# Two fused transformer blocks: the first FFN's up outputs in pairs by Strassen's scheme

## The chip, the cores and the metric

The kernel is one program on one core of a Trainium2 chip. The core has TensorE (matmuls, in the profile PE, with its weight loads as PEld), VectorE (DVE), ScalarE (ACT), GpSimd (POOL) and SyncE (SP), each with its own queue of instructions that it works off in order. They share SBUF; matmuls write to PSUM, which has eight banks of 128 partitions x 512 fp32 numbers. The metric is the device time of one execution in microseconds (us), and lower is better.

## The reference, cut to what matters

Two transformer blocks in float32 on 512 tokens of width 1024, one behind the other. The change touches the FFN of the first block and the last addition of the second:

```python
h2 = rms_norm(x, norm2_w[l])
x = x + jnp.square(jax.nn.relu(h2 @ ffn_w1[l])) @ ffn_w2[l]      # first block: 1024 -> 4096 -> 1024
...
f = (jax.nn.silu(h @ ffn_w_gate[l]) * (h @ ffn_w_up[l])) @ ffn_w_down[l]
x = x + rmsnorm(f, norm_ffn_post[l])                             # second block, the end of the program
```

`rms_norm` divides each token by the root of the mean square over its 1024 channels and multiplies by a gain per channel.

## The kernel before, in words

**Three passes.** Activations lie with channels on the partitions and tokens in the columns, in chunks of 128 channels: `x_sb` is eight chunks of 128 x 512. A float32 product is made of three fast ones. Each operand is split into a high part (a rounded copy, type fp32r) and a low part (the original minus the high one), and `mm3` issues high x high, high x low, low x high into one bank (L834 is the line of every matmul).

**Weights.** SyncE loads slots of 128 x 1024 into `w_raw` (three buffers). GpSimd writes the high part of a slot (L2512) and the low part (L2517, in this part of the program in four pieces of 256 columns) into a ring of three slots, `w_hi_t` and `w_lo_t`. A slot is split once TensorE has finished with the slot three before it (`BEHIND`), and raw buffers come free with the low part.

**The first FFN.** It runs in two halves of 16 chunks. An up chunk (`fm(("up1", half, c))`) takes one slot: 8 channel blocks x 3 passes = 24 matmuls of 512 columns. Its input is not normed: `u2_hi` and `u2_lo` hold x times the gain, and the factor of each token, `r_h`, is multiplied in when the bank is emptied, on VectorE with the ReLU (L2007, into `r1`, whose two chunks take turns). ScalarE squares (L1561) and writes the high part `hid1_hi` (L1562), VectorE the low part `hid1_lo` (`hidden_low`, L1857). Behind 16 up chunks stand eight down chunks (`down1`), each 16 blocks x 3 passes over two slots, which VectorE adds to `x_sb` (L2090).

**The end.** The last FFN ends with eight down chunks summed in `merged_t` (called `f_acc`), the last one in two parts in one bank. Then come the sum of squares through a matmul with ones, logarithm and exponential on ScalarE (L1473, L1476, by token halves), VectorE's product with gain and factor (L2420), the addition to x on TensorE, VectorE and GpSimd, and the DMAs of the result.

**What sets the order.** `plan()` writes one list of steps, `ORDER`. The block of each engine walks through that list and issues its own part of each step, so the order on an engine is the order of the list and of the code of a step. Engines meet by semaphores: `did(...)` counts up behind an instruction, `after(...)` gives the value to wait for, and `own` is a wait on a result of the same engine. `take` picks the bank that has been filled longest ago and waits until it is empty; `release` says so.

## Time and profile before

| | us |
|---|---|
| median of 3 runs | 1781.65 |
| the runs | 1780.2 to 1781.75 |
| the profiled execution, its own time | 1781.87 |
| its span, first to last instruction | 1780.1 |

| engine | busy us | share of the span |
|---|---|---|
| TensorE, matmuls | 1758.4 | 99% |
| GpSimd | 1118.7 | 63% |
| VectorE | 753.0 | 42% |
| ScalarE | 491.5 | 28% |

The mean granted TensorE clock is 0.999 of full speed. Durations of single matmuls overlap, so what one costs is read from the distance of their starts. The profile puts helper functions under one line, and buffer numbers are left out of names: `hid_lo` is `hid1_lo`, `u_hi` is `u2_hi`, `r` is `r1`, `bank` is any of the eight.

### The profile page before, as it was taken

The page shows a single profiled execution, that of the slowest core. Times are in us where ns is not written, and L with a number is a line of the kernel's source. Part 1 is how long each engine was busy: PE and PEld are TensorE (multiplying, and loading weights), DVE is VectorE, ACT ScalarE, POOL GpSimd, SP SyncE. Part 2 cuts the span into 40 slices and gives each one's busy share as a digit, 9 for nine tenths or more (in the row PEclk, how much of TensorE's full clock was granted, in tenths as well). Part 3 has the DMA queues.
Part 4 walks back from the last instruction along what each step waited for, and adds up shares of the span by engine and source line. Part 5 has one row for each costly group of instructions (what it writes and reads, how often), then busy time and mean ns, then how long its engine had stood idle before and what let it go on. Part 6 is the DMA issues. An engine that isn't in the chain of part 4 may idle for free.

```text
span 1780.1 us, 22414 instructions
## 1 busy us (share of the span) xinstructions
PE 1758.4 (99%) x8502; PEld 1417.1 (80%) x8502; DVE 753.0 (42%) x1266; ACT 491.5 (28%) x937; POOL 1118.7 (63%) x1181
## 2 busy tenths in 40 slices
PE   8999999999999999999999999999999999999998
PEld 5776768888888887878888888777888888888886
DVE  6348656320122244262006373545433586215532
ACT  3236653210021111222014232554300222222222
POOL 6643648777777786667766665555788574444442
PEclk9999999999999999999999999999999999999999
DMA  6620012332222223222232222212223232222331
GB/s 218 209 74 28 25 56 99 100 102 95 95 95 96 97 83 126 73 82 96 95 99 74 77 75 83 72 61 71 83 95 107 71 107 95 95 95 96 100 100 59
DMA packets 47001, 162.88 MB, mean 91 GB/s; under 512 B 5582, under 2 KB 6670, under 8 KB 46640
## 3 DMA queue, kind: packets, MB, share of 16 engines
q1 hardware_dynamic: 45688, 158.28, 26.6%
q10 hardware_dynamic: 1208, 3.18, 0.6%
q8 instruction: 68, 1.11, 0.3%
q14 instruction: 37, 0.30, 0.1%
HBM read 158.41 MB, written 2.11 MB: 90 GB/s over the span
## 4 chain that ended last, share of the span: by engine, by line
PE 93%; DVE 3%; ACT 1%; issue 1%; DMA 0%; POOL 0%; ACTq 0%; SPq 0%; DVEq 0%; POOLq 0%
PE bank L834 92%; DVE sq_sum L1847 1%; PE bank L1222 1%; PE bank L1176 1%; DMA x_sb<-in_x 0%; DVE tmp L1852 0%; DVE h_lo L1910 0%; ACT sq L1435 0%; POOL w_lo_t L2517 0%; ACT att_pt L1693 0%; ACT att_l_t L1680 0%; DVE sq_parts L1880 0%; ACT h_hi L1547 0%; ACT sb_e L1752 0%; DVE tmp L2215 0%
## 5 line engine op out<-in xcount | busy, mean ns | idle before, releaser
L2517 POOL TENSOR_TENSOR w_lo_t<-w_raw,w_hi_t 128x256 fp32r<-128x256 f32 (+1 forms) x892 | 820.8, 948 | 168.2 <-ACT w_hi_t L1513 149.8
L2512 POOL TENSOR_SCALAR w_hi_t<-w_raw 128x1024 fp32r<-128x1024 f32 (+1 forms) x221 | 241.2, 1091 | 430.6 <-PE bank L834 395.2
L834 PE MATMUL bank<-h_hi,w_hi_t 128*128 128x512 f32 x1044 | 418.6, 401 | 9.3 <-ACT h_hi L1547 8.5
L834 PE MATMUL bank<-h_hi,w_lo_t 128*128 128x512 f32 x1044 | 407.4, 390 | 0.0
L834 PE MATMUL bank<-h_lo,w_hi_t 128*128 128x512 f32 x1044 | 402.8, 389 | 0.2 <-DVE h_lo L1910 0.2
L834 PEld LDWEIGHTS bank<-h_hi,w_hi_t 128*128 128x128 f32 x1044 | 197.0, 189 | 61.7 <-issue 19.9
L834 PEld LDWEIGHTS bank<-h_lo,w_hi_t 128*128 128x128 f32 x1044 | 195.8, 188 | 42.6 <-issue 1.7
L834 PEld LDWEIGHTS bank<-h_hi,w_lo_t 128*128 128x128 f32 x1044 | 197.1, 189 | 40.7 <-issue 1.2
L834 PE MATMUL bank<-hid_hi,w_hi_t 128*128 128x512 f32 x432 | 168.0, 389 | 0.0
L834 PE MATMUL bank<-hid_lo,w_hi_t 128*128 128x512 f32 x432 | 168.0, 389 | 0.0
L834 PE MATMUL bank<-hid_hi,w_lo_t 128*128 128x512 f32 x432 | 168.0, 389 | 0.0
L834 PE MATMUL bank<-u_hi,w_hi_t 128*128 128x512 f32 x280 | 108.9, 389 | 0.0
L834 PE MATMUL bank<-u_hi,w_lo_t 128*128 128x512 f32 x280 | 108.9, 389 | 0.0
L834 PE MATMUL bank<-u_lo,w_hi_t 128*128 128x512 f32 x280 | 108.9, 389 | 0.0
L1513 ACT ACTIVATE w_hi_t<-w_raw 128x1024 fp32r<-128x1024 f32 x52 | 55.0, 1060 | 187.6 <-PE bank L834 187.5
L834 PEld LDWEIGHTS bank<-hid_hi,w_hi_t 128*128 128x128 f32 x432 | 81.1, 188 | 17.0
L834 PEld LDWEIGHTS bank<-hid_lo,w_hi_t 128*128 128x128 f32 x432 | 81.1, 188 | 16.8
L834 PEld LDWEIGHTS bank<-hid_hi,w_lo_t 128*128 128x128 f32 x432 | 81.1, 188 | 16.8
L1561 ACT ACTIVATE r<-r 128x512 f32<-128x512 f32 x32 | 20.2, 632 | 214.9 <-DVE r L2007 214.9
L834 PE MATMUL bank<-o_hi,w_hi_t 128*128 128x512 f32 x192 | 75.8, 395 | 0.0
L834 PE MATMUL bank<-o_lo,w_hi_t 128*128 128x512 f32 x192 | 74.8, 390 | 0.0
L834 PE MATMUL bank<-o_hi,w_lo_t 128*128 128x512 f32 x192 | 74.8, 390 | 0.0
(364 smaller groups left out, 2509.9 us busy)
## 6 DMA issues: line engine op xcount, KB each, us to landing
w_raw<-in_w SPq DMA_DIRECT2D x276, 512.0 KB, 3.2
y<-in_w SPq DMA_DIRECT2D x6, 512.0 KB, 4.8
x_sb<-in_x SPq DMA_DIRECT2D x4, 512.0 KB, 7.5
out_y<-x_sb SPq DMA_DIRECT2D x8, 256.0 KB, 2.4
x_sb<-in_x ACTq DMA_DIRECT2D x1, 1536.0 KB, 6.8
u_raw<-in_w SPq DMA_DIRECT2D x2, 512.0 KB, 5.9
toep<-table SPq DMA_DIRECT2D x4, 256.0 KB
decay<-in_decay SPq DMA_DIRECT2D x1, 1024.0 KB, 4.9
```

The costliest lines, as they stand in the source:

```text
L834: return pe.matmul(out, lhs, rhs, start=start, stop=stop, **kw)
L1176: last = pe.transpose(out[:, b * P:(b + 1) * P], att_row(u)[0][:, b * P:(b + 1) * P], ident[:])
L1222: last = pe.transpose(out[:, 256 * hf + b * P:256 * hf + (b + 1) * P], row[:, b * P:(b + 1) * P], ident[:])
L1513: act.activation(w_hi[RING[i]], w_raw[:, n % RAW], ACT.Copy).then_inc(*did("wa_hi", i))
L1561: chain(act.activation(r1[:, n % 2], r1[:, n % 2], ACT.Square))
L1847: dve.tensor_tensor(sq_sum[0:parts, 0:cols], b[0] if c == 1 else sq_sum[0:parts, 0:cols], b[1], ALU.add).then_inc(*did("sq_v", key, c))
L2512: pool.tensor_scalar(hi[:, 0:cols], raw[:, 0:cols], 1.0, 0.0, ALU.mult, ALU.add).then_inc(*did("w_hi", i))
L2517: ins = pool.tensor_tensor(lo[:, piece], raw[:, piece], hi.bitcast(F32)[:, piece], ALU.subtract)
```

## The change

**Alone and in pairs.** The first eight up chunks of half 0 stay as they are (`N_ALONE`). The other 8 of half 0 and all 16 of half 1 are made two at a time: four pairs and eight pairs. A pair's output is two chunks x 512 tokens, seen as 2 x 2 quarters: upper and lower chunk, left and right 256 tokens. The input is seen as 2 x 2 as well, channels 0 to 511 and 512 to 1023 by token halves, and so is the weight. By the form of Strassen's scheme used here, seven products of quarters do instead of eight. A product is 4 blocks x 3 passes = 12 matmuls of 256 columns.

**Inputs.** Sums of inputs need real, normed ones, since the token factor differs from left to right. VectorE writes `x_norm` (`st_norm`), four sums `x_sums` of it (`st_sum`), and ScalarE and VectorE split them (`st_split`) into `h_hi` and `h_lo`. Three plain input quarters are split behind the last single chunk (`st_x`, `st_x_rest`). All of this stands between the single chunks 2 to 7 and in front of the first pair.

**Weights.** Four of the seven products use sums of weight quarters. VectorE makes them in four banks (`sums`), ScalarE writes their high parts (`sum_hi`), VectorE their low parts (`sum_lo`). The three plain quarters are split by GpSimd (`raw_quarter`). The ring is now counted in half slots (`place_weights`); a fourth raw buffer `w_more` is used for pairs.

**Outputs.** ScalarE copies the first product out (`pair_p6`). VectorE adds the third to it (`u2_t`), adds the second (`q_t`), and the three quarters `pair_c22`, `pair_c12`, `pair_c21`; the fifth, sixth and seventh products add onto banks that these have read. ScalarE makes the ReLU, square and copy of each chunk (`pair_left`, `pair_right`), GpSimd the low part (`hidden_low`), which VectorE made before; the last pair's stand between the first down slots.

**The end of the program.** The last down chunk is done by token halves in two banks (`down_halves`), so that the left half's norm and addition are issued while TensorE works on the right half.

```diff
     for half in range(2):
-        for c in range(half == 0, HALF1):
+        alone = range(1, N_ALONE) if half == 0 else ()
+        for c in alone:
+            if c == N_ALONE - 1:
+                run([("st_pre", ("pair", 0, N_ALONE)), ("st_x",)])
             fm(("up1", half, c))
+            run([("st_" + what,) for what, at in (("norm", 2), ("sum", 3), ("split", 4)) if c == at])
+        if half == 0:
+            put(("st_x_rest",))
+        for c in range(N_ALONE * (half == 0), HALF1, 2):
+            lin(("pair", half, c), "pair", 2)
         down(("down1", half), HALF1, "pre")
+        if half == 0:
+            order.insert(len(order) - 1, ("st_pre", ("pair", 1, 0)))
...
+    Q_S2, Q_S1, Q_W11, Q_S3, Q_W12, Q_S4, Q_W22 = range(7)
+    X_OF = {Q_S2: T2, Q_S1: T1, Q_W11: X11, Q_S3: T3, Q_W12: X21, Q_S4: X22, Q_W22: T4}
+    BANK_OF = {Q_S2: "b", Q_S1: "c", Q_W11: "a", Q_S3: "d", Q_W12: "a", Q_S4: "c", Q_W22: "d"}
...
+            elif stage == "pair":
+                name = step[1]
+                for m in range(7):
+                    x, spot = X_OF[m], (name, BANK_OF[m])
+                    out = (take(spot) if m < 4 else ps(spot))[:, 0:T // 2]
+                    pe.wait_ge(*after("st_lo" if m in (Q_S1, Q_S2, Q_S3, Q_S4) else "w_lo", name, m))
+                    if m == Q_W12:
+                        pe.wait_ge(*after("st_u2", name))
+                    elif m == Q_S4:
+                        pe.wait_ge(*after("st_q", name))
+                    elif m == Q_W22:
+                        pe.wait_ge(*after("st_c22", name))
...
+                    for k in range(4):
+                        wsl = slice(k * P, (k + 1) * P)
+                        xh, xl = x_quarter(k, x)
+                        last = mm3(out, wh[:, wsl], wl[:, wsl], xh, xl, k == 0 and m < 4, k == 3, skip_group_check=True)
...
+        def sum_hi(name, s):
+            m = Q_OF_S[s]
+            act.wait_ge(*after("st_s", name, {1: 2, 2: 4, 3: 3, 4: 4}[s]))
+            act.wait_ge(*slot_done[BEHIND[(name, m)]])
+            act.activation(quarter(name, m)[0], s_of(name, s), ACT.Copy).then_inc(*did("st_hi", name, m))
...
+        def pair_phase(pairs):
+            sum_hi(pairs[0], 4)
+            for old, new in zip(pairs, pairs[1:]):
+                pair_p6(old)
+                sum_hi(new, 2)
+                sum_hi(new, 1)
+                sum_hi(new, 3)
+                pair_left(old)
+                sum_hi(new, 4)
+                pair_right(old)
...
+        def pair_inner(name):
+            dve.wait_ge(*after("st_pe", name, Q_W11))
+            dve.wait_ge(*evacuated((name, "b")))
+            dve.tensor_tensor(u2_t, pair_bank(name, "a"), p6_t, ALU.add).then_inc(*did("st_u2", name))
+            own("st_u2", name)
+            dve.tensor_tensor(q_t, u2_t, pair_bank(name, "c"), ALU.add).then_inc(*did("st_q", name))
...
+            for old, new in zip(pairs, pairs[1:]):
+                sums(new)
+                sum_lo(new, 2)
+                pair_inner(old)
+                sum_lo(new, 1)
+                pair_c22(old)
+                sum_lo(new, 3)
+                pair_c12(old)
+                pair_c21(old)
+                sum_lo(new, 4)
...
+            since += 1
+            if n and PAIR_SLOT[i] is not None and since in (2, 3):
+                hidden_low(PAIR_SLOT[i], since - 2)
...
+                for hf, chunks in enumerate((range(KD), (0, 1, 4, 2, 5, 3, 6, 7))):
+                    side = halves_t[hf]
+                    own("rstd", "fpost", hf)
+                    for c in chunks:
+                        if c == KD - 1:
+                            dve.wait_ge(*after("last_c", hf))
+                        dve.scalar_tensor_tensor(out=f_acc[:, c, side], in0=f_acc[:, c, side], scalar=col("fpost", c),
+                                                 in1=ps(("ms", "fpost", hf))[:, 0:T // 2], op0=ALU.mult, op1=ALU.mult)\
+                           .then_inc(*did("last_t", hf, c))
```

VectorE, from the bank of single chunk 2 on. In the kernel before, each chunk has two instructions:

```order
L2007 SCALAR_TENSOR_TENSOR r<-bank,r_h 128x512 [waits bank_full7,hid]
L1857 TENSOR_TENSOR hid_lo<-r,hid_hi 128x512 [waits hid_s]
L2007 SCALAR_TENSOR_TENSOR r<-bank,r_h 128x512 [waits bank_full6,hid]
L1857 TENSOR_TENSOR hid_lo<-r,hid_hi 128x512 [waits hid_s]
L2007 SCALAR_TENSOR_TENSOR r<-bank,r_h 128x512 [waits bank_full3,hid]
```

The same place in the changed kernel, up to the low parts of the input sums:

```order
L2364 SCALAR_TENSOR_TENSOR r<-bank,r_h 128x512 [waits bank_full7,hid]
L2099 TENSOR_TENSOR hid_lo<-r,hid_hi 128x512 [waits hid_s]
L2094 SCALAR_TENSOR_TENSOR x_norm<-x_sb,par,r_h 128x512 [waits hid]
L2094 SCALAR_TENSOR_TENSOR x_norm<-x_sb,par,r_h 128x512 x7
L2364 SCALAR_TENSOR_TENSOR r<-bank,r_h 128x512 [waits bank_full6]
L2099 TENSOR_TENSOR hid_lo<-r,hid_hi 128x512 [waits hid_s]
L2217 TENSOR_TENSOR x_sums<-x_norm 128x1024 [waits st_h,hid]
L2217 TENSOR_TENSOR x_sums<-x_norm 128x1024
L2217 TENSOR_TENSOR x_sums<-x_norm,x_sums 128x1024 [waits st_t] x2
L2364 SCALAR_TENSOR_TENSOR r<-bank,r_h 128x512 [waits bank_full3]
L2099 TENSOR_TENSOR hid_lo<-r,hid_hi 128x512 [waits hid_s]
L2221 TENSOR_TENSOR h_lo<-x_sums,h_hi 128x1024 [waits st_xhi,hid]
```

The norms, sums and low parts of the input stand between the chunks' own instructions, and all later ones of VectorE come behind them.

VectorE in one round of the pairs, in the changed kernel, with buffer numbers. Banks 0, 5, 1 and 7 hold the sums of weights; banks 4, 2, 6 and 3 hold the products; `st_pe` counts products of TensorE:

```order
L2123 TENSOR_TENSOR bank0<-w_raw 128x512 [waits st_lo,w_landed2]
L2125 TENSOR_TENSOR bank5<-bank0,w_raw 128x512 [waits st_lo,st_s,w_landed0]
L2127 TENSOR_TENSOR bank1<-w_raw,bank5 128x512 [waits st_lo,st_s]
L2129 TENSOR_TENSOR bank7<-w_raw,bank5 128x512 [waits st_lo]
L2136 TENSOR_TENSOR w_lo_t<-bank5,w_hi_t 128x512 [waits st_hi]
L2144 TENSOR_TENSOR tmp<-bank4,tmp 128x256 [waits bank_free3,st_pe]
L2146 TENSOR_TENSOR tmp<-tmp,bank2 128x256 [waits st_u2]
L2136 TENSOR_TENSOR w_lo_t<-bank0,w_hi_t 128x512 [waits st_hi]
L2152 TENSOR_TENSOR r1<-tmp,bank6 128x256 [waits st_q,st_pe,hid]
L2136 TENSOR_TENSOR w_lo_t<-bank1,w_hi_t 128x512 [waits st_hi]
L2157 TENSOR_TENSOR r1<-tmp,bank2 128x256 [waits st_pe,hid]
L2161 TENSOR_TENSOR r1<-tmp,bank6 128x256 [waits st_pe]
```

The four sums of the next pair (the first four rows) stand in front of the inner sum of the running pair (`tmp<-bank4,tmp`), for which the fifth product waits.

ScalarE in the same round, changed kernel. `w_hi_t<-bank` are the high parts of the next pair's sums, `r` and `hid_hi` belong to the running pair:

```order
L1724 ACTIVATE tmp<-bank 128x256 [waits st_pe,st_u2]
L1700 ACTIVATE w_hi_t<-bank 128x512 [waits st_pe,st_s] x3
L1705 ACTIVATE r<-bank 128x256 [waits st_pe,hid_p]
L1707 ACTIVATE r<-r 128x256 [waits bank_free2]
L1709 ACTIVATE r<-r 128x512 [waits bank_free4,s_chain]
L1710 ACTIVATE hid_hi<-r 128x512 [waits s_chain]
L1700 ACTIVATE w_hi_t<-bank 128x512 [waits st_pe,st_s]
L1714 ACTIVATE r<-r 128x512 [waits bank_free6]
L1715 ACTIVATE r<-r 128x512 [waits s_chain]
L1716 ACTIVATE hid_hi<-r 128x512 [waits s_chain]
```

The high part of the fourth sum stands behind the four instructions of the running pair's left chunk; before the change ScalarE had two instructions per up chunk, and none on weights here.

## Rows read from the trace of the kernel before

**Rows 1.** The page: busy times of the engines

```profile
PE 1758.4 (99%) x8502; PEld 1417.1 (80%) x8502; DVE 753.0 (42%) x1266; ACT 491.5 (28%) x937; POOL 1118.7 (63%) x1181
```

**Rows 2.** The chain that ended last: start us, us, what

```profile
278.22 511.89 PE bank L834 x2240
...
1767.74 0.48 ACT rstd_t L1473
...
1775.50 0.60 ACT x_sb L1803
```

**Rows 3.** Timeline, TensorE, 512 columns: start us, us, engine, line, names, shapes

```profile
340.00 0.39 PE L834 MATMUL bank<-u_hi,w_hi_t 128*128 128x512 f32 x1
...
343.85 0.39 PE L834 MATMUL bank<-u_hi,w_lo_t 128*128 128x512 f32 x1
...
349.07 0.39 PE L834 MATMUL bank<-u_lo,w_hi_t 128*128 128x512 f32 x1
```

**Rows 4.** Timeline, TensorE, 256 columns

```profile
1397.05 0.28 PE L834 MATMUL bank<-m_hi,w_lo_t 128*128 128x256 f32 x1
...
1398.85 0.28 PE L834 MATMUL bank<-m_hi,w_lo_t 128*128 128x256 f32 x1
```

**Rows 5.** Timeline, VectorE: up outputs of chunks 2 and 7 leave their banks

```profile
317.50 0.69 DVE L2007 SCALAR_TENSOR_TENSOR r<-bank,r_h 128x512 f32<-128x512 f32 x1 [4.15 <-PE bank L834]
...
344.35 0.69 DVE L2007 SCALAR_TENSOR_TENSOR r<-bank,r_h 128x512 f32<-128x512 f32 x1 [3.80 <-PE bank L834]
```

**Rows 6.** Groups of VectorE by shape, 278 to 790 us: busy, mean ns

```profile
L1857 DVE TENSOR_TENSOR hid_lo<-r,hid_hi 128x512 fp32r<-128x512 f32 x32 | 32.8, 1025 | 0.7 <-ACT hid_hi L1562 0.7
...
L2007 DVE SCALAR_TENSOR_TENSOR r<-bank,r_h 128x512 f32<-128x512 f32 x32 | 22.1, 692 | 122.0 <-PE bank L834 119.5 <-ACT r_h L1496 2.5
...
L2319 DVE TENSOR_TENSOR ret_a_t<-bank,decay 128x256 f32<-128x256 f32 x3 | 1.2, 415 | 0.0
```

**Rows 7.** Groups of ScalarE by shape, same stretch

```profile
L1561 ACT ACTIVATE r<-r 128x512 f32<-128x512 f32 x32 | 20.2, 632 | 214.9 <-DVE r L2007 214.9
...
L1581 ACT ACTIVATE sig<-bank 128x512 f32<-128x512 f32 x6 | 3.6, 598 | 64.2 <-PE bank L834 64.2
```

**Rows 8.** Groups of GpSimd by shape, whole span

```profile
L2517 POOL TENSOR_TENSOR w_lo_t<-w_raw,w_hi_t 128x256 fp32r<-128x256 f32 x826 | 651.0, 818 | 17.3
...
L2512 POOL TENSOR_SCALAR w_hi_t<-w_raw 128x1024 fp32r<-128x1024 f32 x220 | 240.6, 1094 | 425.5 <-PE bank L834 395.2 <-DVE h_lo L1910 20.9 <-DMA w_raw<-in_w 9.3
...
L2512 POOL TENSOR_SCALAR w_hi_t<-w_raw 128x512 fp32r<-128x512 f32 x1 | 0.6, 617 | 5.1 <-DMA w_raw<-in_w 5.1
```

**Rows 9.** Busy time of each engine, 656.27 to 676.00 us

```profile
core 0: us, PE busy (x) PEld busy (x) DVE busy (x) ACT busy (x) POOL busy (x), PEclk, DMA share, GB/s
656.27:676.00 19.73, 19.73 (x89) 16.34 (x88) 19.03 (x17) 6.34 (x9) 18.45 (x18) 1.00 0.40 148
```

**Rows 10.** Timeline, GpSimd: a weight slot split beside an idle and a busy VectorE

```profile
644.74 2.82 POOL L2517 TENSOR_TENSOR w_lo_t<-w_raw,w_hi_t 128x256 fp32r<-128x256 f32 x4
...
661.75 4.49 POOL L2517 TENSOR_TENSOR w_lo_t<-w_raw,w_hi_t 128x256 fp32r<-128x256 f32 x4
...
666.20 1.50 POOL L2512 TENSOR_SCALAR w_hi_t<-w_raw 128x1024 fp32r<-128x1024 f32 x1
```

**Rows 11.** Timeline, ScalarE, end of the program

```profile
1768.24 0.42 ACT L1476 ACTIVATE rstd_t<-rstd_t 128x256 f32<-128x256 f32 x1
```

**Rows 12.** Timeline, VectorE, end of the program

```profile
1768.69 0.48 DVE L2420 SCALAR_TENSOR_TENSOR sig<-merged_t,par,rstd_t 128x256 f32<-128x256 f32 x1 [7.71 <-ACT rstd_t L1476]
...
1774.65 0.69 DVE L2426 TENSOR_TENSOR x_sb<-x_sb,bank 128x512 f32<-128x512 f32 x1
```

**Rows 13.** Timeline, TensorE, behind a gap

```profile
234.83 1.25 PE L1176 MATMUL bank<-ident,x_sb 128*128 128x128 f32 x8 [2.20 <-DVE x_sb L2217]
```

**Rows 14.** TensorE behind that gap: stretch, its length, busy, granted clock

```profile
237.00:238.00 1.00, 1.00 (x7) 0.50 0.06 16
...
240.00:241.00 1.00, 1.00 (x8) 1.00 0.00 0
```

More of the change, by code:

```diff
@@ L47 @@
 RAW = 3
+N_ALONE = 8
 SPL = 3
@@ L366 @@
             LAST_USE[SLOTS[name][0]] = n
+    elif step[0] == "pair":
+        LAST_USE.update({(step[1], m): n for m in range(7)})
     elif step[0] == "down":
@@ L722, in h_free @@
                 last = (step[2], NT - 1)
-        if last is not None:
+            elif step[0] == "pair":
+                last = step[1]
+        if last in PAIR_LIST:
+            eng.wait_ge(*after("st_pe", last, 6))
+        elif last is not None:
             eng.wait_ge(*full(last))
@@ L915, in _ @@
                     fill(("tab", n), mm(out[0:NH, :], rb[rows], onehot[rows], True, True))
-            elif stage == "norm" and step[1] != "post":
+            elif stage == "norm" and step[1] not in ("post", "fpost"):
                 ms(step[1], len(norms[step[1]][0]))
@@ L1060, in _ @@
                 nm = (name[0], name[1], o)
[L1061 to L1066 removed]
+                if name[0] == "down2" and o == KD - 1:
+                    down_halves(nm, nk, i0)
+                    continue
+                out = take(nm)
                 for k in range(nk):
@@ new lines, in sum_lo, with pair_bank @@
+        def sum_lo(name, s):
+            m = Q_OF_S[s]
+            own("st_hi", name, m)
+            hi, lo = quarter(name, m)
+            dve.tensor_tensor(lo, s_of(name, s), hi.bitcast(F32), ALU.subtract).then_inc(*did("st_lo", name, m))
+        def pair_bank(name, b):
+            return ps((name, b))[:, 0:T // 2]
+        def pair_inner(name):
[4 more added lines that the diff above has]
+            dve.tensor_tensor(q_t, u2_t, pair_bank(name, "c"), ALU.add).then_inc(*did("st_q", name))
@@ L1861, in _, with x_lo @@
+        def x_lo(n):
+            c0, side = (X11, X21, X22)[n]
+            own("st_xhi", n)
+            blocks = [(0, 4, u2_lo05[:, 0:4])] if c0 == 0 else [(4, 6, u2_lo05[:, 4:6]), (6, 8, u2_lo67[:])]
+            for k0, k1, lo in blocks:
+                ins = dve.tensor_tensor(lo[:, :, side], h_norm[:, k0:k1, side], u2_hi[:, k0:k1, side].bitcast(F32),
+                                        ALU.subtract)
+            ins.then_inc(*did("st_xlo", n))
         for i, v in enumerate(EPS_VAL):
@@ L2551, in _ @@
             name = step[1]
-            if stage in ("fm", "tm", "cmp_up", "out_end") or (stage == "down" and step[3] == 0):
+            if stage in ("fm", "tm", "cmp_up", "out_end", "pair") or (stage == "down" and step[3] == 0):
                 first, count = SLOTS[name]
```

450 lines of the change are left out of this document (358 added, 92 removed).

## The prediction

> **What bounds the kernel now.** I read the page first: TensorE is busy for 99% of the span, the other engines for 28 to 63% [rows 1]. The reader is to see that TensorE work taken away is time taken away, as long as nobody makes TensorE wait. The chain of waits says the same of the stretch in question: from 278.22 us it runs through 511.89 us of matmuls without a break [rows 2], and the whole first FFN (up chunks and down chunks) lies inside. So the change is worth the matmul time it removes, minus every wait that it puts into a stretch that has none today. The program then ends with a piece that is not TensorE: from 1767.74 us the chain is ScalarE and VectorE work on the last norm, and its last piece begins at 1775.50 us [rows 2].
>
> Next I took prices. Matmuls of 512 columns start 9.07 us apart over 40 intervals (340.00 to 349.07), which is 0.227 us each [rows 3]. Matmuls of 256 columns start 1.80 us apart over 15 intervals, 0.120 us each, and not half of 0.227 [rows 4]. Both streams are at full clock. A part of about 0.013 us per matmul does not shrink with the columns.
>
> **The pairs on TensorE.** Two up chunks are 48 matmuls of 512 columns, 48 x 0.227 = 10.88 us. A pair is 7 products x 4 blocks x 3 passes = 84 matmuls of 256 columns, 84 x 0.120 = 10.08 us (1.44 us a product). The gain is 0.80 us a pair, 7% and not an eighth. With 12 pairs that is 9.6 us, if nothing waits. The Trainium skill (TensorE: Matmul & The Clock Gate, section Back-to-back issue gap) gives columns / 2.4 + 2.5 ns, which would be 0.109 and 0.216 us and 1.2 us a pair. The trace has 0.120 and 0.227, and the sum goes by those.
>
> **The loop through the pairs.** What stands between pairs is a ring through three engines, and I price it from rows. A VectorE instruction of 512 columns that reads a bank takes 0.69 us and one of 256 columns 0.415; one that reads two SBUF tensors beside a busy GpSimd takes 1.03 on average [rows 6]. ScalarE takes 0.63 from SBUF and 0.60 from a bank for 512 columns [rows 7], and 0.42 for 256 [rows 11]. A result of TensorE is taken up 0.27 us after the next matmul could have started: the last matmul of chunk 7 starts at 343.85, the next is due at 344.08, and VectorE begins at 344.35 [rows 3, 5]. Other hand-overs I take at 0.04.
> From the order of the instructions: when the sixth product (S4) of a pair ends, VectorE makes the upper right quarter (0.27 + 0.42). ScalarE then does ReLU 0.42, square 0.63 and copy 0.63, and only behind these the high part of the next pair's fourth sum, 0.60: 2.4 us with hand-overs. VectorE takes its low part (0.69) and then makes the four sums of the pair after that, which depend on each other: about 1.0 + 3 x 0.69 = 3.1. ScalarE takes the high part of the second sum (0.64, it waits for the fourth), VectorE its low part (0.72), and only then the inner sum of the running pair (0.42), for which the fifth product waits. Fifth and sixth product follow, 2.88. Round trip: 0.69 + 2.4 + 0.73 + 3.1 + 0.68 + 0.72 + 0.44 + 0.16 + 2.88 = 11.8 us. A pair can't be faster than this ring, so in steady state it takes 11.8 us against 10.88 before: **0.9 us lost a pair**, where TensorE alone would win 0.8. Four pairs have two such rounds and eight have six; the first and last pair of a phase are outside. The price of the write of a sum into a bank is in no row; with 0.69 for every sum the ring is 11.5, with 1.0 for every sum 12.7. I take 11.8, since three of the four read only one SBUF tensor.
> GpSimd would not be worse than that: per pair three quarters (0.62 + 2 x 0.71 to 0.82 each) and two low parts of the hidden (2 x 0.71 to 0.82 each) [rows 8, 10] are 9.0 to 10.1 us with nothing added, inside 11.8.
>
> **The set-up before the first pair.** This is the largest term. Today VectorE has only 0.69 + 1.03 us in 5.44 us of each up chunk [rows 5, 6]. The changed kernel puts between chunks 2 and 7: eight normed chunks, four sums and four low parts of 1024 columns, four weight sums and three low parts, in front of the chunks' own work. VectorE is then a queue without a gap while GpSimd splits weights, and a later stretch shows what that means: 17 instructions in 19.03 us, 1.12 each, both engines busy nearly throughout [rows 9]; in such a stretch GpSimd's four pieces take 4.49 instead of 2.82 [rows 10]. A 1024-column instruction stands in no row: 256 columns cost 0.415 and 512 cost 0.69, so 1.25 alone, and 1.68 with one wait of 0.43 for GpSimd; two of 1.12 would be 2.24. I take 1.68, since it follows the two shapes that have rows. The Trainium skill (SBUF — State Buffer, section SBUF: two separate sides) says that the loser of the shared ports waits for a whole instruction of the winner, which gives one wait and 1.68; a shared rate would give 2.24, and the eight would cost 4.5 us more. No row here decides between them.
> From 317.50 [rows 5]: bank and low part 1.81, norms 8 x 1.12 = 9.0, 1.81, sums 6.7, 1.81, low parts 6.7, 3.6, which is 348.9. Weight sums 2.8 (GpSimd is idle by then), ScalarE 0.64, low part 0.7: 353.1. TensorE has finished chunk 7 at 344.1, so the first product is **9.0 us late**. The next three products run to 358.9. VectorE meanwhile: two low parts 1.4, first input quarter 1.5, bank and low part of chunks 7 and 6 1.4, four more pieces 2.8, 0.7, low part 0.7, the next pair's sums 2.8, ScalarE 0.64, 0.7, inner sum 0.42: 366.1. The fifth product is **7.2 us late**. A gap also costs clock: after a wait of 2.20 us [rows 13] the granted clock was 0.50 in 237 to 238 us and 1.00 again in 240 to 241 [rows 14], i.e. 1.2 GHz for some 3.5 us. Behind the second gap that is 1.7 us more; behind the first it disappears in the second.
>
> **The ends of the phases.** The hidden low parts of the last pair go to GpSimd, between the first down slots. GpSimd comes out of the ring 6.9 us after the last pair's start, splits a slot in 4.2 (1.05 + 4 x 0.78), and TensorE is due at 10.1: about 1.2 us late. Then come one slot, one hidden part (1.6), one slot, and the other hidden part: 23.2, where TensorE needs it at 11.4 + 45 x 0.227 = 21.6. Together 2.9 us a phase, 0 at the least.
>
> **The tail.** The last down chunk of both halves has 66 matmuls of 256 columns instead of 33 of 512: 7.92 for 7.48, so 0.9 us more. In return the left half's norm is done before TensorE ends: VectorE needs 8 x 0.42 + 0.43 = 3.8 us behind its factor instead of 6.65 (1768.69 to 1775.34) [rows 12], and ScalarE has two instructions instead of four ahead of that (0.85). Net -2.5; bounds -4 and +0.9.
>
> **Sum.** First phase: 9.0 + 7.2 + 1.7 + 2 x 0.92 - 2 x 0.80 + 2.9 = 21.0. Second phase: sums wait for the last down chunk, first pair 1.1 late, so +0.3, then 6 x 0.92 - 0.80 + 2.9: 7.9 in all. Tail -2.5. Together +26.4 on the profiled execution's 1781.87 us (span 1780.1): 1808.3. The median of the runs is 1781.65, so I forecast 1808.
>
> **Rivals.**
> Faster (1770): the ring does not bind, since VectorE and ScalarE have slack on average (VectorE has some 8 us in 10.08), and the set-up hides. Then 12 x 0.80 + 2.5 are won, 1769.8. For it: those averages, and five products of lead in the weight buffers. Against it: averages do not shorten a chain, and the order puts the next pair's sums in front of the running pair's inner sum. It decides if the ring is below 10.1 us and VectorE's queue ends before 344.
> Only the set-up costs (1788): pairs run at 10.08, ends cost nothing, +17.9 - 9.6 - 2.5 = +5.8.
> No contention in the set-up (1799): at 0.69 and 1.25 VectorE's queue is done at 344, the 9.0 us vanish, 1808 - 9. Against it: the 1.12 us of such a stretch [rows 9].
> Clock (1822): every wait of 1.1 to 1.8 us in the pairs lowers TensorE to 1.2 GHz as the one of 2.20 did [rows 13, 14]. The products behind it are on the ring, 8 x 1.7 more.
>
> **How the numbers follow.** Forecast 0.50, no contention 0.17, only the set-up 0.10, clock 0.08, faster 0.12, and 0.03 that gains and losses cancel. A measurement can tell 0.2% (3.6 us) from no change. Faster by more 0.12, within 0.03, slower 0.85. The range takes in all the slower cases: from 1788 up to 1824, the top being the clock case with a little contention on top. Without the slower cases' spread the forecast's own range is 1800 to 1816.
>
> **What would show it.** In the profile after: VectorE without a gap from 318 to about 366 us; TensorE waiting twice behind it there, for w_lo_t and for tmp, 9 and 7 us; then once in nearly each pair, 1.8 us, for tmp; pairs 11.8 us apart, products of twelve matmuls 1.44 us long; a wait for hid_lo by GpSimd at the first down chunk. Wrong if pairs stand 10.1 us apart (the ring), if the first product starts by 345 us (contention), or if VectorE's 1024-column instructions take over 2 us.

## The result, and the profile after

| | before | after |
|---|---|---|
| median, us | 1780.93 (1779.7 to 1781.75, 4 runs) | 1801.87 (1800.25 to 1802.46, 4 runs) |
| ratio | | 1.0115, 95% interval 1.0103 to 1.0127 |
| profiled execution, span, us | 1780.1 | 1800.2 |

The change makes the kernel slower by 20.9 us. The forecast was 1808, 26.4 over its profiled execution. The page after, against [rows 1]:

```profile
PE 1755.1 (97%) x9000; PEld 1438.0 (80%) x9000; DVE 831.2 (46%) x1404; ACT 541.4 (30%) x1040; POOL 1143.9 (64%) x1223
```

The reader is to see that TensorE's busy time fell by only 3.3 us while its share fell from 99 to 97%: the loss is waiting. Who is waited for shows in TensorE's waits (us in total, times, longest):

```profile
PE bank L953 <- issue: 13.8, 2, 8.3
PE bank L953 <- DVE tmp L2144: 9.5, 9, 1.2
```

**The set-up.** The two "issue" waits are those ahead of the first pair's first and fifth product. (A figure in brackets behind a row is the idle time just before it, by the profile; waits taken from the distance of two starts come out 0.1 to 0.3 us longer.) The last matmul of chunk 7 starts at 345.23 (343.85 before, [rows 3]; 1.4 us of offset arose earlier in the program and is in every number from here on). TensorE was due with the first product at 345.46 and, after four products, with the fifth at 361.59:

```profile
353.91 0.55 PE L953 MATMUL bank<-h_hi,w_hi_t 128*128 128x256 f32 x1 [8.29 <-issue]
...
367.22 0.55 PE L953 MATMUL bank<-u_hi,w_hi_t 128*128 128x256 f32 x1 [5.47 <-issue]
```

"Issue" names nobody, since TensorE waits here for something that ended just before. VectorE's timeline of the same stretch names it:

```profile
320.21 9.44 DVE L2094 SCALAR_TENSOR_TENSOR x_norm<-x_sb,par,r_h 128x512 f32<-128x512 f32 x8
...
330.88 3.63 DVE L2217 TENSOR_TENSOR x_sums<-x_norm 128x1024 f32<-128x1024 f32 x2
334.43 3.44 DVE L2217 TENSOR_TENSOR x_sums<-x_norm,x_sums 128x1024 f32<-128x1024 f32 x2
...
340.86 5.72 DVE L2221 TENSOR_TENSOR h_lo<-x_sums,h_hi 128x1024 fp32r<-128x1024 f32 x4 [1.79 <-ACT h_hi L1749]
...
353.12 1.89 DVE L2136 TENSOR_TENSOR w_lo_t<-bank,w_hi_t 128x512 fp32r<-128x512 f32 x3 [0.66 <-ACT w_hi_t L1700]
355.04 1.23 DVE L2188 TENSOR_TENSOR u_lo<-x_norm,u_hi 128x1024 fp32r<-128x1024 f32 x1
...
357.50 3.88 DVE L2188 TENSOR_TENSOR u_lo<-x_norm,u_hi 128x512 fp32r<-128x512 f32 x4
...
366.09 0.69 DVE L2136 TENSOR_TENSOR w_lo_t<-bank,w_hi_t 128x512 fp32r<-128x512 f32 x1 [0.66 <-ACT w_hi_t L1700]
366.70 0.41 DVE L2144 TENSOR_TENSOR tmp<-bank,tmp 128x256 f32<-128x256 f32 x1
```

Apart from waits for ScalarE of 1.79, 0.66 and 0.66 us VectorE works from 318.9 to 367. The 1.79 us are a loop of its own: ScalarE writes the high parts of the input sums (`h_hi`) only from 339.71, behind a square and a copy of a single chunk whose bank VectorE itself had emptied at 337.80, late. The first low part that TensorE needs begins at 353.12, the inner sum `tmp` of the fifth product at 366.70.

**The ring.** Eight of the waits for `tmp` are 1.13 to 1.16 us and the ninth, at the start of phase 2, is 0.4. One round of VectorE, from one inner sum to the next:

```profile
534.24 0.41 DVE L2144 TENSOR_TENSOR tmp<-bank,tmp 128x256 f32<-128x256 f32 x1
...
538.02 0.42 DVE L2157 TENSOR_TENSOR r<-tmp,bank 128x256 f32<-128x256 f32 x1
...
540.81 0.69 DVE L2136 TENSOR_TENSOR w_lo_t<-bank,w_hi_t 128x512 fp32r<-128x512 f32 x1 [1.00 <-ACT w_hi_t L1700]
541.42 0.87 DVE L2123 TENSOR_TENSOR bank<-w_raw 128x512 f32<-128x512 f32 x1
...
543.72 0.69 DVE L2129 TENSOR_TENSOR bank<-w_raw,bank 128x512 f32<-128x512 f32 x1
545.08 0.69 DVE L2136 TENSOR_TENSOR w_lo_t<-bank,w_hi_t 128x512 fp32r<-128x512 f32 x1 [0.66 <-ACT w_hi_t L1700]
545.68 0.41 DVE L2144 TENSOR_TENSOR tmp<-bank,tmp 128x256 f32<-128x256 f32 x1
```

It takes 545.68 - 534.24 = 11.44 us, with the members in the order that the prediction gave them. TensorE's own 84 matmuls would take 10.08, so each round costs 1.36 us.

**The balance**, by marks in the two traces (the start of the same instruction in both), after against before: 1.4 us of offset ahead of the change; phase 1 (chunk 7's last matmul to the first down matmul) 61.4 against 43.8, +17.6; phase 2 89.4 against 87.0, +2.4; behind the phases about +0.7. The last long run of matmuls starts at 1461.32 and not 1439.21, 22.1 later, and the span ends 20.1 later: the tail gives 2.0. Without the offset the change costs 18.7 us by these marks (17.6 + 2.4 + 0.7 - 2.0). Its chain after ends so (start us, us, what):

```profile
1461.32 326.08 PE bank L953 x1487
1788.41 3.22 DVE merged_t L2768 x8
1791.63 1.29 DVE x_sb L2773 x2
1792.93 3.14 DVE merged_t L2768 x8
```

### The profile page after: what moved, and what is told of

Same layout as the page of the kernel before. It is cut to its first block, busy times and chain, and to the rows that moved or that the text cites. A ratio compares the mean times of both kernels' runs of the same rounds, so it can differ in the third digit from the quotient of the medians.

```text
span 1800.2 us, 23932 instructions
## 1 busy us (share of the span) xinstructions
PE 1755.1 (97%) x9000; PEld 1438.0 (80%) x9000; DVE 831.2 (46%) x1404; ACT 541.4 (30%) x1040; POOL 1143.9 (64%) x1223
## 3 DMA queue, kind: packets, MB, share of 16 engines
q8 instruction: 72, 1.18, 0.3%
## 4 chain that ended last, share of the span: by engine, by line
PE 64%; DVE 2%; POOL 1%; ACT 0%; issue 0%; DVEq 0%; ACTq 0%; POOLq 0%
PE bank L953 64%; DVE sq_sum L2089 1%; PE bank L1406 1%; POOL w_lo_t L2901 0%; DVE merged_t L2768 0%; POOL hid_lo L2852 0%; DVE tmp L2094 0%; POOL w_hi_t L2896 0%; DVE h_lo L2267 0%; DVE sq_parts L2237 0%; DVE x_sb L2773 0%; ACT sq L1615 0%; PE bank L1513 0%; POOL w_lo_t L2845 0%; DVE x_sb L2799 0%
## 5 line engine op out<-in xcount | busy, mean ns | idle before, releaser
L2901 POOL TENSOR_TENSOR w_lo_t<-w_raw,w_hi_t 128x256 fp32r<-128x256 f32 (+1 forms) x796 | 750.7, 971 | 167.0 <-ACT w_hi_t L1745 150.5
L953 PE MATMUL bank<-h_hi,w_hi_t 128*128 128x512 f32 (+1 forms) x1236 | 473.7, 383 | 17.4 <-ACT h_hi L1792 8.5
L953 PE MATMUL bank<-h_hi,w_lo_t 128*128 128x512 f32 (+1 forms) x1236 | 462.2, 374 | 0.0
L953 PE MATMUL bank<-h_lo,w_hi_t 128*128 128x512 f32 (+1 forms) x1236 | 457.9, 373 | 0.3 <-DVE h_lo L2267 0.3
L953 PE MATMUL bank<-hid_hi,w_hi_t 128*128 128x512 f32 (+1 forms) x454 | 172.5, 380 | 0.3
L953 PE MATMUL bank<-hid_hi,w_lo_t 128*128 128x512 f32 (+1 forms) x454 | 172.0, 379 | 0.0
L953 PE MATMUL bank<-hid_lo,w_hi_t 128*128 128x512 f32 (+1 forms) x454 | 172.0, 379 | 0.0
L953 PE MATMUL bank<-u_hi,w_hi_t 128*128 128x256 f32 (+1 forms) x232 | 76.7, 331 | 14.9 <-DVE tmp L2144 9.5
L953 PE MATMUL bank<-u_lo,w_hi_t 128*128 128x256 f32 (+1 forms) x232 | 75.9, 327 | 0.0
L953 PE MATMUL bank<-u_hi,w_lo_t 128*128 128x256 f32 (+1 forms) x232 | 75.8, 327 | 0.0
```

The source lines that it names most:

```text
L953: return pe.matmul(out, lhs, rhs, start=start, stop=stop, **kw)
L2901: ins = pool.tensor_tensor(lo[:, piece], src[:, piece], hi.bitcast(F32)[:, piece], ALU.subtract)
```

## The experiments

Where a run's profile is compared with another, distances between marks inside the program are used: the place of chunk 7's end differs by up to 3.3 us between the profiled executions, for reasons ahead of the change. "The 1787 kernel" is the first one below. All ratios are to the kernel before, beside runs of it on the same chip.

**1. VectorE's inner sum ahead of the low part (r1_dve).**

```diff
                 sums(new)
-                sum_lo(new, 2)
                 pair_inner(old)
+                sum_lo(new, 2)
```

> Edit: in a round of the pairs VectorE makes the inner sum of the running pair (tmp<-bank,tmp and the q behind it) before the low part of the next pair's second weight sum, not behind it. Ring theory (the round of 11.44 us is a ring: fourth weight sum's low part, four sums of the next pair, high part, low part, inner sum, fifth product, and back through ScalarE's left chunk): the wait for the high part and the low part (0.66 + 0.6 us) leave the ring, so its period falls from 11.44 to about 10.17 us, the same in all 9 rounds, and the gap before the first pair's fifth product shrinks by the same 1.27. Sum: 10 x 1.27 = 12.7 us off 1801.9, so 1789 us. Rival 1 (the round is bound by GpSimd, which splits three quarters and makes two low parts of the hidden activations per pair): period stays 11.4, time 1801 to 1802. Rival 2 (matmuls of 256 columns issue slower than 0.120 us over a long stretch): the same, no wait for tmp left but the distance of the starts grows.

1786.98 us, ratio 1.0031 (1.0019 to 1.0043). The same round in its profile:

```profile
532.15 0.42 DVE L2144 TENSOR_TENSOR tmp<-bank,tmp 128x256 f32<-128x256 f32 x1
...
534.14 0.41 DVE L2152 TENSOR_TENSOR r<-tmp,bank 128x256 f32<-128x256 f32 x1
```

The instruction at L2152 stands at 524.07 one round earlier, so a pair takes 10.07 us. No wait for `tmp` is left, and phase 2 takes 80.7 us, which is eight pairs at TensorE's own 10.08. The wait ahead of the first pair's fifth product fell too, by 1.6 us (distance 4.15 instead of 5.75; 1.27 was expected). The ring theory holds; GpSimd and the matmuls' rate fall as causes, since neither was touched.

**2. ScalarE's fourth high part first (r2_act), and 3. both edits (r3_both).**

```diff
-                pair_left(old)
                 sum_hi(new, 4)
+                pair_left(old)
                 pair_right(old)
```

> Edit: ScalarE writes the high part of the next pair's fourth weight sum before the running pair's left chunk (ReLU, ReLU, square, copy), not behind it. Ring theory: the high part then waits only for the seventh product, which frees its half slot 4.88 us behind the inner sum, instead of 5.89 us: the period falls by about 1.0 us to 10.4 to 10.5 us, and 9 rounds give 9 us: 1793 us. The first pair gains nothing. GpSimd rival: no change, 1802 us. Rival: the left chunk is now so late that its bank or r1 holds up a product; then a new wait of TensorE for bank a (the third product of the next pair) shows, and the time stays above 1797.

1800.67 us, ratio 1.0111 (1.0094 to 1.0127): far less than expected. The rounds take 10.96 us and not 10.4. ScalarE in one of them:

```profile
524.32 0.60 ACT L1700 ACTIVATE w_hi_t<-bank 128x512 fp32r<-128x512 f32 x1 [2.28 <-PE bank L953]
524.81 0.38 ACT L1705 ACTIVATE r<-bank 128x256 f32<-128x256 f32 x1
...
528.58 0.36 ACT L1724 ACTIVATE tmp<-bank 128x256 f32<-128x256 f32 x1
528.84 1.08 ACT L1700 ACTIVATE w_hi_t<-bank 128x512 fp32r<-128x512 f32 x2
```

The high part starts early, but then both chunks' ReLUs, squares and copies, 4.0 us from 524.81 to 528.84, stand between it and the next high part, for which VectorE waits (its sums are ready at 528.4). One ring was shortened and another, through ScalarE's queue, took its place 0.5 us below. There is a second cost: GpSimd's low parts of the hidden chunks wait for ScalarE's later copies (1.82 us, in front of 394.93), and the first down slot stands behind them. The slot is ready at 403.77, and TensorE starts with it at 403.88, 1.7 us late.

> Edit: both edits of the two kernels before. Ring theory: the ring is 11.44 - 1.27 - 1.0 = 9.2 us, shorter than the 84 matmuls of a pair at 0.120 us (10.08 us), so TensorE is the bound: period 10.08, no wait for tmp; 9 x 1.36 + 1.27 = 13.5 us off 1801.9, so 1788.4 us, and phase 2 (eight pairs) takes 80.6 us and not 89.4. If it does not reach 10.08, another ring (GpSimd's quarters, or ScalarE's left chunk and its bank) is behind this one, and its wait shows in TensorE's timeline.

1791.14 us, ratio 1.0058 (1.0043 to 1.0073). 1788.4 was expected. The pairs stand at 10.08 as expected, but that needed the first edit alone; what the second adds is the late down slot, 1.7 and 1.8 us at the ends of the two phases (distances 1.83 and 1.96 between the last and the first matmul, against 0.14). So this is slower than the first edit alone.

**4. The tail alone (tail_only).** The changed kernel with

```diff
+        for c in range(half == 0, HALF1):
+            fm(("up1", half, c))
+        down(("down1", half), HALF1, "pre")
```

in place of the loop with pairs, and VectorE's `hidden_low` of the last chunk put back.

> Edit: the changed kernel with all up chunks of the first FFN single as before (no pairs, no sums of inputs or weights); of the change only the last output chunk by token halves is left. Theory (the two parts add up): the pairs cost 23 us net and the tail gives 2.0 back, so this is 1780.9 - 2.0 = 1778.9 us, ratio 0.9989. Rival (the tail gives nothing or costs, and the pairs' net is only 20.9): 1780.9 us or more. Rival (tail gives the 2.5 us that the prediction's sum had): 1778.4 us. The profile should have TensorE at 0.227 us a matmul in the first FFN, and the last instruction 2 us earlier than before.

1779.7 us, ratio 0.9990 (0.9981 to 0.9999). From the start of the last long run of matmuls to the end of the span it takes 1778.1 - 1439.03 = 339.1 us, and before 1780.1 - 1439.21 = 340.9: 1.8 us, against 2.0 in the whole change, so the two parts add up within 0.2 us. The pairs' net is then 1801.9 - 1779.7 = 22 us.

**5. Less GpSimd beside the set-up (c1_quiet).** Three quarters of the low parts of the weights of chunks 3 to 7 are left out:

```diff
-            for k in range(0, cols if n == 0 else 1024, size):
+            quiet = i in [SLOTS[("up1", 0, c)][0] for c in range(3, N_ALONE)]
+            for k in range(0, cols if n == 0 else size if quiet else 1024, size):
```

> Edit: the changed kernel, with GpSimd writing only the first 256 of 1024 columns of the low parts of the weights of single chunks 3 to 7 (three quarters of that part of the computation are left out), so that it is idle for most of the time in which VectorE prepares the inputs. Contention theory (VectorE's instructions with two SBUF operands take 1.18 us, and 1.77 us with 1024 columns, because GpSimd works beside them): the eight normed chunks fall from 1.18 to about 0.70 us each and the four sums from 1.77 to about 1.3, 5.7 us less in VectorE's queue, and the wait of TensorE in front of the first pair falls from 8.7 to about 3 us: 1801.9 - 6 = 1796. Rival (the operations take this long by themselves; the queue alone makes the wait): durations and the wait stay, 1802.

1795.97 us, ratio 1.0083 (1.0070 to 1.0097), 5.9 us less. VectorE's added work in its timeline:

```profile
318.66 7.02 DVE L2094 SCALAR_TENSOR_TENSOR x_norm<-x_sb,par,r_h 128x512 f32<-128x512 f32 x8
...
326.91 3.21 DVE L2217 TENSOR_TENSOR x_sums<-x_norm 128x1024 f32<-128x1024 f32 x2
330.04 3.01 DVE L2217 TENSOR_TENSOR x_sums<-x_norm,x_sums 128x1024 f32<-128x1024 f32 x2
...
336.03 5.05 DVE L2221 TENSOR_TENSOR h_lo<-x_sums,h_hi 128x1024 fp32r<-128x1024 f32 x4 [1.78 <-ACT h_hi L1749]
```

2.4, 0.8 and 0.7 us less than after, 3.9 in all, and the first product comes 4.3 us earlier against chunk 7's end (4.4 instead of 8.7). Contention is real, and the part of it that this edit takes away is about half of that wait. It did not go away altogether (0.88 a norm and not 0.70), as GpSimd still writes high parts and the first pieces, so half is the least that contention costs here. What the wait would be with none is not shown: an estimate from the durations, 8 norms at 0.69, 4 sums and 4 low parts at 1.23 (what these shapes take where GpSimd is idle), has VectorE's queue 6.9 us shorter than after, which would leave some 1.6 us of the 8.45. The second wait grew from 5.75 to 6.4, and phase 1 has 4.3 us less in all; the other 1.6 us of the medians' difference no mark explains.

**6. Normed inputs earlier (s1r_early),** on the 1787 kernel:

```diff
+        if half == 0:
+            put(("st_norm",))
         for c in alone:
...
-            run([... for what, at in (("norm", 2), ("sum", 3), ("split", 4)) if c == at])
+            run([... for what, at in (("sum", 2), ("split", 3)) if c == at])
```

> Edit, on top of the kernel with VectorE's inner sum ahead of the low part (1787): the normed inputs are made behind single chunk 0 and not 2; the sums stay behind chunk 2, the split moves from chunk 4 to 3. Queue theory (the first pair is late because VectorE has 22 us of added work in its queue between chunk 2 and the end of chunk 7, while it is idle 3.4 and 4.2 us ahead of the banks of chunks 1 and 2): some 7 us of the work go into that idle time, the wait ahead of the first pair falls from 8.7 to 1 to 3 us, and the fifth product, whose inputs stand in the same queue, comes 7 to 9 us earlier too: 1787 - 8 = 1779. Rival (the end of chunk 7 sets the time, by the plain input quarters which may only be written then, and the weights' landing): the first pair starts earlier, but the fifth product hardly does, and the total falls by under 3 us.

1783.06 us, ratio 1.0011 (1.0002 to 1.0020), 3.9 less; half of what was expected. TensorE's waits in its timeline:

```profile
340.78 0.50 PE L955 MATMUL bank<-u_hi,w_hi_t 128*128 128x512 f32 x1 [1.34 <-POOL w_lo_t L2903]
347.85 0.36 PE L955 MATMUL bank<-h_hi,w_hi_t 128*128 128x256 f32 x1 [1.30 <-issue]
360.33 0.56 PE L955 MATMUL bank<-u_hi,w_hi_t 128*128 128x256 f32 x1 [6.49 <-DVE tmp L2146]
```

The first pair's wait is nearly gone, as the queue theory says: the first product comes 7.0 us earlier against chunk 7's end than in the 1787 kernel (distance 1.69 instead of 8.66). A new wait appears ahead of chunk 7: now GpSimd is the one that is held up, and its weight slot is 1.5 us late. The fifth product waits 6.5, but it too comes 6.8 us earlier against chunk 7's end (14.2 behind it and not 21.0), so the rival, by which it would hardly move, was wrong. It waits longer because the four products ahead of it came earlier still and ran at the full clock (5.7 us from first to last start and not 8.2). What it waits for is VectorE again, which works without a gap from the first low part at 347.06 to the inner sum at 359.81; the low parts of the plain input quarters are 5.1 us of that. By the marks phase 1 is 6.2 us shorter and chunk 7 is 1.5 late, 4.7 in all against 3.9 by the medians.

**7. The first inner sum ahead of the second pair's sums (s2r_inner),** on the 1787 kernel, in the first round only:

```diff
+                if old == PAIR_LIST[0]:
+                    pair_inner(old)
                 sums(new)
-                pair_inner(old)
+                if old != PAIR_LIST[0]:
+                    pair_inner(old)
                 sum_lo(new, 2)
```

> Edit, on top of the kernel with 1787: in the first round alone VectorE makes the first pair's inner sum ahead of the four weight sums of the second pair. Queue theory: the fifth product comes 2.9 us earlier (four sums of 0.7), and the second pair's first product, whose sums are now later, gives 0.3 back: 1787 - 2.6 = 1784.4, with the wait ahead of the first pair unchanged at 8.7. Rival (the fifth product waits for the plain input quarters or for the weight quarter of GpSimd): under 1 us less, 1786 or more.

1786.57 us, ratio 1.0036 (1.0022 to 1.0050): nothing gained. The fifth product's wait fell by 3.0 us, from a distance of 4.15 to 1.12, and the seventh's came in its place:

```profile
360.53 0.36 PE L953 MATMUL bank<-u_hi,w_hi_t 128*128 128x256 f32 x1 [0.84 <-issue]
...
366.35 0.36 PE L953 MATMUL bank<-h_hi,w_hi_t 128*128 128x256 f32 x1 [2.72 <-POOL w_lo_t L2848]
```

The profile names GpSimd, but the seventh product's weights had long been split (at 357.6; what GpSimd finished at 365.91 belongs to the second pair). VectorE made the quarter that frees the seventh product's bank at 365.84, 0.41 us long, behind the second pair's sums and two of its low parts. The expectation had followed the second pair and forgotten the bank that the first one still needed.

**8. All of it (s4_all),** on the 1787 kernel: experiment 6, the first weight sums ahead of chunk 6, the third input quarter's low part on GpSimd, and the first round of VectorE in the order of need:

```diff
+            if start:
+                pair_inner(pairs[0])
             sum_lo(pairs[0], 4)
+            if start:
+                hidden_low(0, N_ALONE - 1)
+                pair_c22(pairs[0])
...
```

> Edit, on top of the kernel with 1787: normed inputs behind chunk 0, sums behind 2, split behind 3, the first pair's weight sums ahead of chunk 6; GpSimd writes the low part of the third plain input quarter; VectorE takes the first round in the order of need (inner sum, low part of the fourth weight sum, low part of chunk 7, c22, then the second pair's sums). Queue theory: the wait ahead of the first pair falls from 8.7 to 0 to 1 us, the one ahead of the fifth product from 4.2 to 0 to 1.5, the second pair is 2 us late, the clock stays at its upper level: from the end of chunk 7 to the first down chunk 43 to 45 us and not 57.1, so 1787 - 13 = 1774 us, 7 under the kernel before (ratio 0.996). Rival (the pairs' gain is lost in any order, since VectorE's work near the end of chunk 7 only moves): over 1781.

1781.05 us, ratio 1.0001 (0.9992 to 1.0010). No wait is left ahead of the first pair (distance 0.22), but there are four smaller ones: 1.5 us ahead of chunk 7 for GpSimd, 2.0 ahead of the third product and 1.4 ahead of the second pair for VectorE's low parts, and 2.0 at the second pair's fifth product. Behind the first of the 2.0 the granted clock was 0.55 for 3 us. From chunk 7's end to the first down chunk it is 48.0 us: 9.1 less than in the 1787 kernel, but not the 43 to 45 expected. Expected were 1774 us, and the rival had over 1781. It holds in part: near chunk 7's end some of VectorE's work moves from one wait to another, and half 0's pairs still cost 5.7 us against single chunks (48.0 against 43.8, and chunk 7 is 1.5 late), which is about what half 1's pairs give back.

**9. Pairs in half 1 alone (h1_only),** on the 1787 kernel. Half 0 is all single chunks; the input sums are made during its first six chunks, and the plain quarters chunk by chunk behind chunk 15:

```diff
+        for c in range(1, HALF1 if half == 0 else 0):
+            fm(("up1", half, c))
+            run([... for what, at in (("norm", 1), ("sum", 3), ("split", 5)) if c == at])
+        if half == 0:
+            put(("st_x",))
+        for c in range(0, HALF1 * half, 2):
+            lin(("pair", half, c), "pair", 2)
...
+                for j in range(12):
+                    if j >= 4:
+                        x_low(j - 4)
...
+                    dve.scalar_tensor_tensor(out=x_piece(j), in0=x_sb[:, c, side], scalar=col("norm2", c), in1=r_h[:, side], ...)
```

> Edit, on top of the kernel with 1787 (inner sum ahead of the low part): half 0 has 16 single chunks as before, and only half 1 is made in pairs. The normed inputs are made behind chunk 1, their sums behind 3 and the split behind 5, with ten single chunks behind them; the three plain input quarters are made behind chunk 15, under the first down chunks, chunk by chunk through tmp. Theory (what the pairs lose is lost at the start of the first pair phase, and a pair phase whose inputs are ready runs at 10.08 us a pair): phase 2 takes 80.7 us instead of the 87.0 of eight times two single chunks, 6.4 less; the tail gives 1.5 to 2.0; a late weight slot under the contention of VectorE's added work costs 0 to 3. Sum: 1781.2 - 6.4 - 1.5 + 1 = 1774 us, range 1772 to 1777, ratio 0.994 to 0.998. Rival (the work in half 0 costs as much wherever it stands, since GpSimd becomes late with the weights): 1779 or more.

**1774.2 us, ratio 0.9966 (0.9952 to 0.9980): faster than both kernels**, by 6.0 us than the one before (by the marks 7.8: phase 2 has 6.3 less, the tail 2.0 less, and 0.5 is lost). Its two stretches, phase 2 and the last FFN (length, busy TensorE, its loads, VectorE, ScalarE, GpSimd, granted clock, DMA share, GB/s):

```profile
474.70:555.40 80.70, 80.70 (x673) 80.66 (x672) 54.04 (x97) 45.18 (x89) 73.52 (x102) 1.00 0.30 99
1433.40:1772.30 338.90, 334.11 (x1532) 278.36 (x1532) 150.87 (x171) 79.95 (x97) 161.83 (x73) 1.00 0.29 94
```

TensorE is busy for all of the 80.70 us (87.04 before), and the last FFN has the tail's 2.0. Of the set-up only 0.5 us ahead of one chunk is left, where the weight slot is late. GpSimd is busy for 73.5 of the 80.7 us, so little room is left below TensorE.

**10. The waits filled with matmuls (k1_filled),** on the changed kernel:

```diff
+                    if name == PAIR_LIST[0] and m in (Q_S2, Q_W12):
+                        if m == Q_W12:
+                            pe.wait_ge(*evacuated((name, "b")))
+                        for _ in range(60 if m == Q_S2 else 40):
+                            mm(ps((name, "b"))[:, 0:T // 2], hid1[0][:, 0, 0:P], hid1[0][:, 0, LEFT], True, True)
```

> Edit: the changed kernel with 60 matmuls of 256 columns ahead of the first pair's first product and 40 ahead of its fifth, on finished data into a free bank and overwritten later; they take 7.2 and 4.8 us and fit into the waits of 8.7 and 5.7 us. Clock theory (behind the waits the matmuls of 256 columns start 0.213 us apart and not 0.120, because the granted clock is at its lower level): with TensorE busy in the waits it stays at the upper level; the four products behind the first wait take 5.8 us and not 7.7, which the second wait takes up, and the 20 slow matmuls behind the second come 2.0 us earlier: 1801.9 - 2.0 = 1799.9 us, ratio to the kernel before 1.0104, and the first down chunk stands 59.4 us behind the end of chunk 7 and not 61.4. Rival (the slow starts come from the operands, just written by other engines, and not from the clock): spacing and time stay as they are, 1801.9.

1798.39 us, ratio 1.0100 (1.0083 to 1.0117). The stretches behind the two waits, first in the changed kernel, then in this one (columns as in 9):

```profile
353.90:361.60 7.70, 7.69 (x48) 7.65 (x48) 7.63 (x10) 5.02 (x8) 3.17 (x3) 0.73 0.06 7
...
367.20:371.50 4.30, 4.28 (x20) 4.30 (x21) 1.96 (x4) 0.87 (x2) 0.00 (x0) 0.50 0.00 0
```

```profile
353.00:361.00 8.00, 8.00 (x69) 8.00 (x68) 7.84 (x11) 2.94 (x5) 6.15 (x6) 1.00 0.37 132
361.00:370.00 9.00, 5.91 (x49) 5.73 (x49) 5.87 (x11) 3.43 (x7) 1.85 (x3) 1.00 0.00 1
```

The clock stays at 1.00, and the matmuls behind both waits start 0.120 us apart. The waits were not filled to the end: 1.1 us stayed idle in the first, and in the second

```profile
364.79 0.36 PE L953 MATMUL bank<-u_hi,w_hi_t 128*128 128x256 f32 x1 [3.09 <-issue]
```

and the clock stayed up all the same. From the fifth product to the first down matmul it takes 37.3 us and not 39.4: 2.1 us are the clock's. The fifth product itself came 0.6 us later against chunk 7's end, so phase 1 has 1.5 less. The operand rival falls: the operands are written by the same engines as before, and the slow starts are gone. The rest of the 3.5 us between the medians is not accounted for.

## Why the prediction was right

**Direction and mechanisms: right.** TensorE's work taken away was real (eight pairs take 80.7 us where 16 single chunks took 87.0, experiments 1 and 9), and chains that its new helpers form put more back. The sum's terms, each against its mark (the fifth product's lateness is counted as the prediction counts it, from four products of 1.44 us behind the first; the wait that TensorE really has there is shorter, since the four ran at the lower clock at first):

| term | forecast | measured |
|---|---|---|
| first product late | 9.0 | 8.45 |
| fifth product late | 7.2 | 7.55 |
| clock behind the second wait | 1.7 | 2.1 |
| ring, a round | 11.8 | 11.44 |
| end of a phase | 2.9 | about 0.4 |
| tail | -2.5 | -1.8 to -2.0 |
| phase 1, with its end | +21.0 | +17.6 and some 0.5 |
| phase 2, with its end | +7.9 | +2.4 and some 0.2 |

- *The set-up* came out within 0.6 us, in part by luck. Norms cost 1.18 each where 1.12 was taken, 1024-column sums 1.77 where 1.68 was, and the wait of 1.79 us for ScalarE's high parts had no place in the sum. Against that the low parts of the sums took 5.7 us and not 6.7, and the single chunks' own instructions 2.0 us less than taken, since their low part was 0.68 in most places and not 1.12: GpSimd did not hold it up there. The same shape with GpSimd idle is the input quarter at 355.04: 1.23, where 1.25 was derived. So beside GpSimd a norm of 512 columns has 0.49 added (1.18 against 0.69) and a sum of 1024 columns 0.54, on average: what is added goes by the instruction and not by the column. (The low parts of 1024 columns, 1.43 each, had less added.) The Trainium skill (SBUF — State Buffer, section SBUF: two separate sides) says that the loser waits for the whole instruction of the winner; by that rule, the trace agrees. The rival "no contention" would have the first product on time. Experiment 5 shows that at least half of that wait is contention.
- *The ring* had the right members and the right rounds, two and six. It was 0.36 us a round too long, 0.12 in each of three places: behind each of the two low parts VectorE's next instruction starts after 0.61 and 0.60 us and not 0.73 and 0.72, and from the first weight sum to the second sum's low part it is 3.66 us (541.42 to 545.08) and not 3.78. Experiment 1 shows the ring by breaking it: 1.36 us a round came back in each of eight rounds.
- *The ends of the phases* are the step that failed. "GpSimd comes out of the ring 6.9 us after the last pair's start, splits a slot in 4.2" had it 1.2 late, and a hidden low part 1.7 late. In the trace after:

```profile
402.52 1.06 POOL L2896 TENSOR_SCALAR w_hi_t<-w_raw 128x1024 fp32r<-128x1024 f32 x1
403.66 2.84 POOL L2901 TENSOR_TENSOR w_lo_t<-w_raw,w_hi_t 128x256 fp32r<-128x256 f32 x4
...
410.40 1.44 POOL L2852 TENSOR_TENSOR hid_lo<-r,hid_hi 128x256 fp32r<-128x256 f32 x2
```

GpSimd comes out of the ring 6.0 us after the last pair's start (at 402.52; the pair starts at 396.5), 0.9 earlier than forecast. From there to the end of the last hidden part it takes 14.6 us and not 16.3: a slot's split takes 3.9 and a hidden part 1.4. VectorE has three instructions of 0.42 us between 402.5 and 418.2, so next to nothing contends. The slot is on time, and the wait for the last hidden part is some 0.3 us. I had priced contention into a stretch that has none, and put the start too late; why GpSimd is out of the ring 0.9 us earlier stays open. The same mechanism does bite when ScalarE's copies come later (experiments 2 and 3: 1.7 and 1.8 us). By the marks the forecast is 7.7 us too high (26.4 against 18.7): this term is 5.0 of it (2 x 2.5) and the ring 2.9 (8 x 0.36); the rest cancels. Against the medians it is 5.5 too high. Two of its sums are also off as written: the figures given for an end (6.9, 4.2, 1.6) add up to 2.4 us of delay and not 2.9, and those given for the tail to -2.8 and not -2.5; with them the forecast would have been 1.3 us lower.
- *Clock at every wait* (1822) fell: behind the ring's waits of 1.1 us the granted clock stays at 1.00 (2.4 GHz) and the next matmuls start 0.120 apart. Behind the waits of 8.3 and 5.5 it is at the lower level, 1.2 GHz, for some 20 matmuls.
- *Only the set-up costs* (1788) is what the first experiment nearly made true by moving one line: 1787.0.

The parts of the change then add up to the 18.7 us of the marks: the pairs' arithmetic -9.6 (12 x 0.80), the rings +10.9 (8 x 1.36), the set-up with its clock some 18, the ends and the first pair of phase 2 some 1.2, the tail -1.8 to -2.0. Open are the up to 2 us by which medians differ more than marks, here and in experiments 5, 9 and 10: no run tells whether they belong to the kernels or to their executions.

## What to carry to other kernels

An operand transformation that saves TensorE work creates two kinds of cost: a one-off preparation, which has to be spread to where the helper engines are idle, and a ring through several engines, whose length counts and not their average load. Write the ring down from the order of the instructions and look for the one that stands ahead of what TensorE waits for without being needed for it: here two exchanged lines were worth 13 us by the marks and 15 by the medians. Use the transformation only where its inputs can be ready in time (half 1, not half 0), and expect a wait that is removed to come back at the next consumer in the same queue unless work leaves the queue.

## What the runs showed of the hardware

- The granted clock after a wait of TensorE (idle time by the profile), over the next 3 us: 1.00 behind 1.1 us (after), 1.3 twice (s1r_early), 1.6 and 1.7 (r2_act) and 1.8 (s4_all, second pair); 0.55 behind 1.9 (s4_all, third product), 0.61 behind 2.7 (s2r_inner), 0.66 behind 3.3 (r3_both), 0.52 behind 3.9 (r1_dve), 0.50 behind 5.5 (after). But it was 1.00 behind the 3.1 us left idle in k1_filled, so the length of the wait alone does not decide, and no run here tells what else does. At the lower level matmuls of 256 columns start 0.213 us apart against 0.120. Filling most of the two waits with matmuls kept the clock at 1.00, and that was worth 2.1 us; in the first wait it was worth nothing, since the second took it up.
- Contention runs both ways. With VectorE's two-operand work moved earlier (s1r_early) its norms took the same 1.18 us each, and GpSimd, whose four pieces take 2.8 us alone [rows 10], took 6.1, 4.1 and 5.1 for them in three slots (6.6 in the changed kernel's longest) and delivered one slot 1.5 us late, though it is busy for only 64% of the span.
- A VectorE addition from SBUF into a bank takes 0.70 us alone and, when both inputs are in SBUF, 0.87 (after) to 1.20 (c1_quiet) in most places beside GpSimd. A row for it did not exist before.
